# Two transformer blocks: the first projections start from columns loaded as such, and the long convolution's tiles are split five and three

## The chip, the cores and the metric

The kernel runs on one core of one Trainium2 chip. The metric is the device time of one execution in microseconds (us). TensorE is PE in the profile (PEld its weight loads), VectorE is DVE, ScalarE is ACT, GpSimd is POOL, and SP issues most DMAs.

## The reference

Two blocks of 256 tokens and width 1024, in fp32. Cut to what the change touches:

```python
# block one
xn = rms_norm(x, norm1_g)                       # x * rsqrt(mean(x^2) + eps) * g
proj = xn @ w_in                                # q, keys and values, g_nsa, conv_b, conv_c, conv_x, gate_a, gate_b
u = conv_c * conv_x
y = causal_conv(u, conv_w)                      # 3 taps, each channel by itself
z = conv_b * y
mixed = sigmoid(gate_a) * (o_nsa @ w_branch_a) + sigmoid(gate_b) * (z @ w_branch_b)
# block two, the branch with the long convolution
u = a * sigmoid(gate)
u = causal_conv(u, conv_w_2) + conv_b_2         # 31 taps, each channel by itself
u = silu(layer_norm(u)); y_conv = u @ w_conv_out
```

## The kernel before

**Products in parts.** Every fp32 product is made of three fp32r ones. ScalarE rounds an operand to fp32r (the hi part, by `copy`, L916), VectorE subtracts it from the original (the lo part, L1435 for weights, L1494 for tokens), and TensorE sums hi x hi, hi x lo and lo x hi (`mm`, L400).

**Units.** All weights come in 302 units of mostly two k-tiles x 512 columns (512 KB), in the fixed order of `units`. SP loads a unit into one of five `raw` buffers as soon as the lo part of the unit five before it is made, ScalarE makes `whi`, VectorE `wlo`, each in rings of five, and TensorE uses them. `rows` puts tokens on the output's partitions (12 matmuls of 512 columns for a unit), `cols` channels (24 of 256 columns). Two to four PSUM banks take a group's tiles; a bank is used again when its tile has been copied out (`bank_free`), by ScalarE for the groups in `by_act` and by VectorE for the others.

**Order.** Each engine runs a program written out by hand. `run(name, ...)` on ScalarE and VectorE makes the hi or lo parts up to four units ahead, and the generators given to it (attention, conv taps, norms) do one step per unit. Engines work in program order, so whatever stands ahead of a hi or lo part delays it.

**The start.** The tokens `X` are loaded first, then unit 0, and TensorE transposes the raw tokens (L404, 16 transposes, zero matmuls before, between and after them). ScalarE and VectorE make the hi and lo parts of these columns times the gain in `OT`. The groups `b1_q`, `b1_kv` (four units of 512 columns each) and `b1_w` (four of 280) run on these unscaled columns, and `copy_out` puts the norm's factor in afterwards, row by row. The factor comes from ScalarE's four squares (L961), VectorE's mean (L1465, L1467) and a power on GpSimd (L2105). VectorE scales the rows into `XS`, and TensorE transposes them too, four transposes after each unit of `b1_kv` (`turn_first`). All later groups of block one (`b1_c0`, `b1_x0`, `b1_c1`, `b1_x1`, `b1_b0`, `b1_b1`, the gates) run on these scaled columns in `XT`.

**Convolution of block one.** ScalarE copies the tiles of `b1_c0` and `b1_c1` out (`copy_col`) into `CC`, and VectorE multiplies the tiles of `b1_x0` and `b1_x1` by them (`col_product`, L1712).

**The long convolution.** Of its eight tiles of 128 channels VectorE makes four (`PE_CONV`), 31 taps each (`taps2`, L1838 and L1842), spread over the units: two taps a unit for 24 units, then three. TensorE makes the other four (`conv_taps`) as 32 matmuls of 32 x 32 tiles each, from a shifted copy `U4` that comes by 16 DMAs, and blocks `WQ` that VectorE makes. One tile is done after every second unit. When all eight are in `YC`, VectorE sums them (L1858), and TensorE needs that sum for the layer norm's mean.

```python
if q == 0: wait_bank(name, f)                             # cols, TensorE, before a tile's first matmul
e.wait_ge(factor, t + 1)                                  # ScalarE, ahead of each copy_out of the first groups
```

## Time and profile before

| what | us |
|---|---|
| runs before: median (lowest to highest of 3) | 943.23 (942.1 to 943.39) |
| the profiled execution, its own time | 942.65 |
| its span, first to last instruction | 940.8 |
| PE busy | 932.1 |
| DVE busy | 671.5 |
| ACT busy | 523.3 |
| POOL busy | 15.2 |

The profiled execution's time is 1.85 us above its span. Busy time is a share of the whole span: PE is busy for 99% of it, DVE for 71%, ACT for 56%, and the mean hides stages in which DVE is busy nearly throughout. The mean DMA rate is 178 GB/s over the span.

### The profile page before, as it was taken

Reading aid. Unit: us, or ns where it says so; the run is one execution under the profiler, and the core shown is the slowest. Engines: PE = TensorE matmul, PEld = TensorE weight load, DVE = VectorE, ACT = ScalarE, POOL = GpSimd, SP = SyncE. Lnnn points to the kernel's source line nnn. Section 1 sums busy time; section 2 is a strip of 40 time slices with the busy share of each in tenths; the row PEclk is TensorE's granted clock in tenths of the full one; section 3 lists DMA queues with packets and bytes.
Section 4 is the critical chain, followed back from the end, with each engine's and each line's share of the span. In section 5 each row is a group of like instructions: output and inputs, shape, how many; then the busy total and the mean of one; then the engine's idle time right before and its main releaser. Section 6 shows DMA issues by size and latency. Waiting matters only on the chain.

```text
span 940.8 us, 14580 instructions
## 1 busy us (share of the span) xinstructions
PE 932.1 (99%) x5619; PEld 802.7 (85%) x5619; DVE 671.5 (71%) x1142; ACT 523.3 (56%) x897; POOL 15.2 (2%) x20
## 2 busy tenths in 40 slices
PE   9999999999999999999999999999999999999997
PEld 7999987788888888889999988888788888888886
DVE  5669976477776666667568876999786676666665
ACT  6655677745654544555444435664855664555453
...
PEclk9999999999999999999999999999999999999999
...
DMA packets 89540, 167.06 MB, mean 178 GB/s; under 512 B 7616, under 2 KB 12416, under 8 KB 89344
## 3 DMA queue, kind: packets, MB, share of 16 engines
...
q14 instruction: 23, 0.19, 0.1%
...
HBM read 162.68 MB, written 1.05 MB: 174 GB/s over the span
## 4 chain that ended last, share of the span: by engine, by line
PE 95%; ACT 2%; DVE 1%; issue 1%; POOLq 0%; POOL 0%; DVEq 0%; ACTq 0%
PE pb L400 92%; PE pb L404 3%; ACT whi L916 1%; ACT YC L1233 0%; DVE LNS L1858 0%; ACT ZO L916 0%; ACT GA L1056 0%; ACT L1233 0%; ACT L1056 0%; DVE GA L1725 0%; DVE XS L2069 0%; ACT S L1372 0%; DVE wlo L1435 0%; ACT GC L1056 0%; DVE ZO L1494 0%
## 5 line engine op out<-in xcount | busy, mean ns | idle before, releaser
L1435 DVE TENSOR_TENSOR wlo<-raw,whi 128x1024 fp32r<-128x1024 f32 (+2 forms) x300 | 357.5, 1213 | 157.3 <-ACT whi L916 156.4
L916 ACT ACTIVATE whi<-raw 128x1024 fp32r<-128x1024 f32 (+2 forms) x302 | 310.2, 1047 | 162.4 <-PE pb L400 147.2
L400 PE MATMUL pb<-XT,whi 128*128 128x256 f32 (+1 forms) x1552 | 372.8, 323 | 0.0
L400 PE MATMUL pb<-XT,wlo 128*128 128x256 f32 (+1 forms) x1032 | 290.6, 282 | 0.0
L400 PEld LDWEIGHTS pb<-XT,whi 128*128 128x128 f32 x1552 | 257.6, 190 | 28.6 <-issue 3.8
L400 PE MATMUL pb<-whi,ZO 128*128 128x512 f32 (+2 forms) x904 | 280.3, 387 | 0.9 <-DVE wlo L1905 0.6
L400 PEld LDWEIGHTS pb<-whi,ZO 128*128 128x128 f32 x904 | 168.4, 188 | 36.4 <-DVE wlo L1435 1.6
L400 PEld LDWEIGHTS pb<-XT,wlo 128*128 128x128 f32 (+1 forms) x1032 | 195.8, 190 | 0.5
L400 PE MATMUL pb<-wlo,ZO 128*128 128x512 f32 (+2 forms) x452 | 173.7, 384 | 0.0
L400 PE MATMUL pb<-whi,XT 128*128 128x512 f32 x448 | 150.8, 401 | 0.0
L400 PEld LDWEIGHTS pb<-whi,XT 128*128 128x128 f32 x448 | 84.2, 188 | 18.3 <-issue 1.3
L400 PEld LDWEIGHTS pb<-wlo,ZO 128*128 128x128 f32 x452 | 85.0, 188 | 16.0
L400 PE MATMUL pb<-wlo,XT 128*128 128x512 f32 x224 | 87.5, 391 | 0.0
L1842 DVE SCALAR_TENSOR_TENSOR YC<-U,PR,YC 128x256 f32<-128x256 f32 x120 | 51.4, 478 | 0.0
L400 PEld LDWEIGHTS pb<-wlo,XT 128*128 128x128 f32 x224 | 42.2, 189 | 7.6
L916 ACT ACTIVATE RT<-pb 128x256 f32<-128x256 f32 x64 | 24.0, 375 | 40.5 <-PE pb L400 40.5
L1762 DVE TENSOR_TENSOR HF<-pb,RT 128x256 f32<-128x256 f32 x64 | 26.9, 420 | 24.8 <-ACT RT L916 24.8
L916 ACT ACTIVATE ZO<-HF 128x256 fp32r<-128x256 f32 x64 | 26.8, 419 | 25.0 <-DVE HF L1765 23.3
L1765 DVE SCALAR_TENSOR_TENSOR HF<-HF 128x256 f32<-128x256 f32 x64 | 27.2, 426 | 2.2
L1754 DVE TENSOR_TENSOR ZO<-HF,ZO 128x256 fp32r<-128x256 f32 x64 | 26.9, 420 | 2.4 <-ACT ZO L916 1.1
L2105 POOL TENSOR_TENSOR ST<-ST,CST 128x1 f32<-128x1 f32 (+3 forms) x14 | 13.7, 986 | 916.5 <-DVE ST L1467 682.5
L1122 ACT ACTIVATE SM<-SM,ST 128x128 f32<-128x128 f32 (+1 forms) x48 | 21.4, 447 | 11.9 <-DVE ST L1581 11.8
...
## 6 DMA issues: line engine op xcount, KB each, us to landing
raw<-in_w_in SPq DMA_DIRECT2D x107, 512.0 KB, 4.2
raw<-in_w_ff SPq DMA_DIRECT2D x64, 512.0 KB, 4.5
raw<-in_w_up SPq DMA_DIRECT2D x32, 512.0 KB, 4.3
raw<-in_w_down SPq DMA_DIRECT2D x32, 512.0 KB, 4.6
raw<-in_w_branch_b SPq DMA_DIRECT2D x8, 512.0 KB, 4.5
raw<-in_w_out SPq DMA_DIRECT2D x8, 512.0 KB, 5.1
raw<-in_wx_kv SPq DMA_DIRECT2D x8, 512.0 KB, 5.0
raw<-in_w_attn_out SPq DMA_DIRECT2D x8, 512.0 KB, 3.5
```

The lines of the kernel that those rows point to most:

```text
L400: return e.matmul(o, l, r, start=start, stop=stop, skip_group_check=True)
L404: return e.transpose(o, s, ident[0:n, 0:n])
L916: return e.activation(o, i, ACT.Copy, scale=scale)
L1122: i = e.activation(SM[j % 4][:, c0:c1], SM[j % 4][:, c0:c1], ACT.Exp, bias=INM[j % 4][:, t:t + 1], scale=post, accum_out=ISM[j % 4][:, t:t ...
L1435: e.tensor_tensor(wlo[u % NW][:, 0:c], raw[u % NRAW][:, 0:c], whi[u % NW][:, 0:c].bitcast(F32), ALU.subtract).then_inc(lo, 1)
L1754: e.tensor_tensor(ZT[:, a + 256:a + 512], HF[:, f, :], ZT[:, a:a + 256].bitcast(F32), ALU.subtract).then_inc(h_lo, 1)
L1762: e.tensor_tensor(HF[:, f, :], PB[bank_of[name, f]][:, 0:256], RT[:, m % 2, :], ALU.add).then_inc(out_d, 1)
L1765: e.scalar_tensor_tensor(out=HF[:, f, :], in0=HF[:, f, :], scalar=0.0, in1=HF[:, f, :], op0=ALU.max, op1=ALU.mult).then_inc(h_sq, 1)
L1842: m = e.scalar_tensor_tensor(out=YC[:, f, :], in0=U2[:, f, k:k + 256], scalar=prm("convw2", 8 * k + f), in1=YC[:, f, :], op0=ALU.mult, op1 ...
L2105: return e.tensor_tensor(dst, src, mhalf(rows, n), ALU.pow)
```

## The change

**The start.** The host also gives the tokens as columns (`xt`). SP loads them in three parts into `XF`, between the first units; `X` itself now comes after unit 4, and the constants come in one piece ahead of unit 4. ScalarE and VectorE make the hi and lo parts in `XT` from `XF`. All 32 transposes of tokens are gone, as are the scaled rows; five zero matmuls are left. For the first three units `first_rows` takes hi and lo parts as they are made. ScalarE squares `X` only after the hi part of unit 6, and then waits for the factor.

**The factor.** Block one runs on unscaled columns throughout. Conv_b and the gates get the factor later (`copy_out` with a scale, `times` with a scalar). Conv_c x conv_x needs it squared, per token, along the columns: VectorE puts 1/mean on diagonals (`DR`), one matmul of 256 columns turns them into rows, and VectorE multiplies the tiles of `b1_c0` and `b1_c1` by them (`RX`) in place of ScalarE's copies. These two groups leave `by_act`, so that their banks now come free by VectorE.

**The long convolution.** VectorE makes five tiles, TensorE three. The taps are spread anew: three a unit for 8 units, two for 15, six for 7, then three; the last step has two in place of one.

```diff
-T_X0, T_X, T_M1, T_MEM, T_2, T_MIX, T_M2, T_XA, T_FFN = range(9)
+T_X, T_M1, T_MEM, T_2, T_MIX, T_M2, T_XA, T_FFN = range(8)
...
-PE_CONV = 4
+SCALED = {n: i for i, n in enumerate((N_MEM, N_MIX))}
+GAIN = {T_X: "norm1", T_MEM: "normmem", T_2: "norm2", T_MIX: "normmix", T_XA: "normx", T_FFN: "normffn"}
+PE_CONV = 5
...
-by_act = {"b1_q", "b1_kv", "b1_w", "b1_c0", "b1_c1", "b1_gb0", "b1_gb1", "b1_ga0", "b1_ga1", "mk", "mv",
+by_act = {"b1_q", "b1_kv", "b1_w", "b1_gb0", "b1_gb1", "b1_ga0", "b1_ga1", "mk", "mv",
...
+    def load_columns(i):
+        a, b = ((0, 512), (512, 1024), (1024, 2048))[i]
+        e.dma_start(XF[:, a:b], A["xt"][:, a:b]).then_inc(xt_in[i], 16)
+
+    load_columns(0)
+    for k in range(2):
+        e.dma_start(raw[0][:, 512 * k:512 * k + 512], units[0][0][0][0][:, k, :]).then_inc(raw_in[0] if k else first_in, 16)
+    load_columns(1)
+    load(1)
+    load_columns(2)
+    load(2)
+    load(3)
+    e.dma_start(CST[:, :], A["consts"]).then_inc(cst_in, 16)
+    load(4)
     for t in range(2):
         e.dma_start(X[:, t * D:t * D + D], xv[:, t, :]).then_inc(x_in[t], 16)
-    for k in range(2):
-        e.dma_start(raw[0][:, 512 * k:512 * k + 512], units[0][0][0][0][:, k, :]).then_inc(raw_in[0] if k else first_in, 16)
-    load(1)
-    e.dma_start(CST[:, 128:CS["end"]], A["consts"][:, 128:CS["end"]]).then_inc(cst_in, 16)
-    for u in range(2, NRAW):
-        load(u)
     e.dma_start(PR[:, 8:NPRM], A["params"][:, 8:NPRM]).then_inc(prm_in, 16)
...
                 e.dma_start(U4[32 * j:32 * j + 32, :, g, a:284],
-                            U2[32 * g:32 * g + 32, 4:8, j + a - 1:j + 283]).then_inc(u4_in, 16)
+                            U2[32 * g:32 * g + 32, PE_CONV:8, j + a - 1:j + 283]).then_inc(u4_in, 16)
...
+    def first_rows(name, T):
+
+        for u in range(count[name] - 1):
+            h, l = weight_tiles(u)
+            for k in range(2):
+                kt = 2 * u + k
+                e.wait_ge(*((first_k, 1) if kt == 0 else (hi, u + 1)))
+                for part in range(2):
+                    e.wait_ge((t_hi, t_lo)[part], kt + 1)
+                    for t in range(2):
+                        a = kt * 512 + part * 256 + t * P
+                        mm(PB[bank_of[name, t]][:, :], T[:, a:a + P], h[:, k, :], kt == 0 and part == 0, False)
+            for k in range(2):
+                kt = 2 * u + k
+                e.wait_ge(*((first_k, 2) if kt == 0 else (lo, u + 1)))
+                for t in range(2):
+                    a = kt * 512 + t * P
+                    i = mm(PB[bank_of[name, t]][:, :], T[:, a:a + P], l[:, k, :], False, False)
+            i.then_inc(unit_done, 1)
...
-    def turn_first():
-        for j in range(4):
-            rows_scaled(N_X, j)
-            turn_tiles(T_X, j, XS, (t_lo, t_at[T_X0, j]))
-            yield
+    def factor_rows():
+        yield
+        yield
+        e.wait_ge(cst_in, 16)
+        e.wait_ge(dr_made, 2)
+        mm(PB[4][:, 0:256], ones, DR[:, :], True, True).then_inc(rx_done, 1)
+        yield
 
...
-        for n in range(4):
+        for n in range(8 - PE_CONV):
...
-    def busy(n):
-        for _ in range(n):
-            mm(PB[3][:, 0:256], DG[:, 0:128], DG[:, 0:256], True, True)
-
     e.wait_ge(zeros, 1)
-    busy(6)
-    e.wait_ge(id_in, 16)
-    for t in range(2):
-        e.wait_ge(x_in[t], 16)
-        for j in range(4):
-            for k in range(2):
-                c = t * D + (2 * j + k) * P
-                i = turn(PB[4 + j][:, k * 256 + t * P:k * 256 + t * P + P], X[:, c:c + P])
-            if t:
-                i.then_inc(turned, 1)
-        busy(1 if t == 0 else 3)
-    side = turn_first()
-    rows("b1_q", OT, t_ready(T_X0))
-    rows("b1_kv", OT, t_ready(T_X0), side)
-    rows("b1_w", OT, t_ready(T_X0))
+    for _ in range(5):
+        mm(PB[3][:, 0:256], DG[:, 0:128], DG[:, 0:256], True, True)
+    first_rows("b1_q", XT)
+    rows("b1_q", XT, t_ready(T_X), begin=3)
+    rows("b1_kv", XT, t_ready(T_X), factor_rows())
+    rows("b1_w", XT, t_ready(T_X))
...
-    make_t_hi(T_X0, 0, OT)
-    for k in range(2):
-        e.wait_ge(raw_in[0] if k else first_in, 16)
-        copy(whi[0][:, 512 * k:512 * k + 512], raw[0][:, 512 * k:512 * k + 512]).then_inc(
-            *((hi, 1) if k else (first_k, 1)))
-    made[0] = 1
-    for j in range(1, 4):
-        make_t_hi(T_X0, j, OT)
-        make_hi()
-    for t in range(2):
-        e.wait_ge(x_in[t], 16)
-        for i in range(2):
-            norm_square(N_X, X, i, t)
+    for j in range(4):
+        e.wait_ge(xt_in[min(j, 2)], 16)
+        for kt in (2 * j, 2 * j + 1):
+            copy(XT[:, kt * 512:kt * 512 + 256], XF[:, kt * 256:kt * 256 + 256], prm(GAIN[T_X], kt)).then_inc(t_hi, 1)
+        for k in range(2) if j == 0 else ():
+            e.wait_ge(raw_in[0] if k else first_in, 16)
+            copy(whi[0][:, 512 * k:512 * k + 512], raw[0][:, 512 * k:512 * k + 512]).then_inc(
+                *((hi, 1) if k else (first_k, 1)))
+        if j == 0:
+            made[0] = 1
+        else:
+            make_hi()
     for n, (name, c0, w) in enumerate((("b1_q", 0, 512), ("b1_kv", 512, 512), ("b1_w", 1024, 280))):
-        run(name, *([turn_first()] if n == 2 else []))
+        run(name)
+        for t in range(2) if n == 0 else ():
+            e.wait_ge(x_in[t], 16)
+            for i in range(2):
+                norm_square(N_X, X, i, t)
         for t in range(2):
             e.wait_ge(factor, t + 1)
             copy_out(name, t, QKV[:, t, c0:c0 + w], NR[N_X][t])
...
     side = attention1()
     for i in range(2):
         run(f"b1_c{i}", side)
-        for f in range(4):
-            if i == 1:
-                e.wait_ge(qk_t, 6)
-            copy_col(f"b1_c{i}", f, CC[i][:, f, :])
         run(f"b1_x{i}", side)
...
-                    copy_out(f"b1_{nm}{i}", t, g)
+                    copy_out(f"b1_{nm}{i}", t, g, NR[N_X][t])
...
+            if n is None:
+                e.tensor_tensor(g, PB[bank_of[name, t]][:, :], g, ALU.mult).then_inc(out_d, 1)
+            else:
+                e.scalar_tensor_tensor(out=g, in0=PB[bank_of[name, t]][:, :], scalar=NR[n][t], in1=g,
+                                       op0=ALU.mult, op1=ALU.mult).then_inc(out_d, 1)
...
     def conv_blocks():
-        for n in range(4):
+        for n in range(8 - PE_CONV):
...
     def taps2():
-        n, made = 0, {}
-        for f0 in range(0, PE_CONV, 2):
+
+        places = itertools.chain(*([q] * n for q, n in enumerate((3,) * 8 + (2,) * 15 + (6,) * 7 + (3,) * 20)))
+        made, at = {}, 0
+        for fs in ((0, 1), (2, 3, 4)):
             for k in range(31):
-                for f in (f0, f0 + 1):
+                for f in fs:
+                    q = next(places)
+                    while at < q:
+                        at += 1
+                        yield
                     if k == 0:
...
-                    n += 1
-                    if n % (2 if n < 48 else 3) == 0:
-                        yield
...
-    make_t_lo(T_X0, 0, OT)
+    def make_x_lo(j):
+        for kt in (2 * j, 2 * j + 1):
+            a = kt * 512
+            e.wait_ge(t_hi, kt + 1)
+            e.scalar_tensor_tensor(out=XT[:, a + 256:a + 512], in0=XF[:, kt * 256:kt * 256 + 256],
+                                   scalar=prm(GAIN[T_X], kt), in1=XT[:, a:a + 256].bitcast(F32), op0=ALU.mult,
+                                   op1=ALU.subtract).then_inc(t_lo, 1)
+
+    make_x_lo(0)
...
-    norm_rows(N_X, X, XS)
     run("b1_q")
+    e.wait_ge(cst_in, 16)
+    for t in range(2):
+        mean(N_X, t, 2 + 2 * t)
+        e.wait_ge(summed, t + 1)
+        step(e.reciprocal(NSUM[N_X][t], NMEAN[N_X][t]))
+        after_step()
+        e.tensor_scalar(DR[:, t * P:t * P + P], ident, NSUM[N_X][t], None, ALU.mult).then_inc(dr_made, 1)
     head_mean(0)
     run("b1_kv")
+    e.wait_ge(rx_done, 1)
+    e.tensor_copy(RX[:, :], PB[4][:, 0:256]).then_inc(rx_out, 1)
     head_mean(1)
     head_scale(0)
-    run("b1_w", turn_first())
+    run("b1_w")
     head_mean(2)
     head_scale(1)
     side = attention1()
     taps = []
     for i in range(2):
         run(f"b1_c{i}", side, *taps)
+        e.wait_ge(*((qk_t, 6) if i else (rx_out, 1)))
+        for f in range(4):
+            col_product(f"b1_c{i}", f, CC[i][:, f, :], RX[:, :])
         run(f"b1_x{i}", side, *taps)
         now(*taps)
...
-    times("b1_wb0", GB, 0, gate_made(2))
+    times("b1_wb0", GB, 0, gate_made(2), N_X)
...
+    xt = I["x"].reshape(256, 8, P).transpose(2, 1, 0).reshape(P, 2048)
+    arrays = {"xt": xt, "params": params, "consts": c, "consts2": c2, "wcmp": wcmp, "x": I["x"], "mem_2": I["mem_2"],
```

ScalarE from the last columns' hi parts on. Before:

```order
L916 ACTIVATE ZO<-pb,PR 128x256 x2
L916 ACTIVATE whi<-raw 128x1024
L961 ACTIVATE XS,ST<-X 128x512 x4
L916 ACTIVATE whi<-raw 128x1024 x3
L916 ACTIVATE QKV<-pb,ST 128x512 x2
L1073 ACTIVATE SQ<-QKV 128x1024
L916 ACTIVATE whi<-raw 128x1024
```

Now (lines are those of the changed kernel):

```order
L940 ACTIVATE XT<-XF,PR 128x256 x2
L940 ACTIVATE whi<-raw 128x1024 x4
L985 ACTIVATE XS,ST<-X 128x512 x4
L940 ACTIVATE QKV<-pb,ST 128x512 x2
L1092 ACTIVATE SQ<-QKV 128x1024
```

The four squares of `X` (output `XS`) moved behind the hi parts of units 4, 5 and 6, to just ahead of the first copies out, which need the factor. The next hi part, that of unit 7, stands behind them as before.

VectorE at the end of `b1_c1` (SM are attention's scores, CC the tiles of conv_c). Before:

```order
L1573 SCALAR_TENSOR_TENSOR SM<-pb,CST 128x384
L1578 TENSOR_REDUCE ST<-SM 128x1 x2
L1581 TENSOR_SCALAR ST<-ST 128x2
L1435 TENSOR_TENSOR wlo<-raw,whi 128x1024
L1698 TENSOR_SCALAR CC<-UU,PR 128x256
```

Now:

```order
L1585 SCALAR_TENSOR_TENSOR SM<-pb,CST 128x384
L1590 TENSOR_REDUCE ST<-SM 128x1 x2
L1593 TENSOR_SCALAR ST<-ST 128x2
L1724 TENSOR_TENSOR CC<-pb,RX 128x256 x4
L1452 TENSOR_TENSOR wlo<-raw,whi 128x1024
```

The four products that release the banks of `b1_c1` stand behind the scores of two heads, and ahead of the next unit's lo part.

VectorE in the units before attention's second part (YC are the taps). Before:

```order
L1842 SCALAR_TENSOR_TENSOR YC<-U,PR,YC 128x256 x2
L1435 TENSOR_TENSOR wlo<-raw,whi 128x1024
L1842 SCALAR_TENSOR_TENSOR YC<-U,PR,YC 128x256 x3
L1435 TENSOR_TENSOR wlo<-raw,whi 128x1024
L1842 SCALAR_TENSOR_TENSOR YC<-U,PR,YC 128x256 x3
```

Now:

```order
L1865 SCALAR_TENSOR_TENSOR YC<-U,PR,YC 128x256 x6
L1452 TENSOR_TENSOR wlo<-raw,whi 128x1024
L1865 SCALAR_TENSOR_TENSOR YC<-U,PR,YC 128x256 x2
L1861 TENSOR_SCALAR YC<-U,PR 128x256 x3
L1865 SCALAR_TENSOR_TENSOR YC<-U,PR,YC 128x256
```

Seven units in a row have six taps each where one had two and six had three.

## Rows read from the trace of the kernel before

**Rows 1.** The page: PE's busy time, and the clock granted in 40 slices.

```profile
PE 932.1 (99%) x5619; PEld 802.7 (85%) x5619; DVE 671.5 (71%) x1142; ACT 523.3 (56%) x897; POOL 15.2 (2%) x20
...
PEclk9999999999999999999999999999999999999999
```

**Rows 2.** Waits of PE: engine line <- releaser: us in total, times, longest.

```profile
PE pb L400 <- DVE wlo L1435: 0.4, 1, 0.4
...
PE pb L400 <- DVE LNS L1858: 0.3, 1, 0.3
```

**Rows 3.** Timeline of PE, first 11 us: start us, us, engine, line, instruction [idle before].

```profile
1.19 5.12 PE L400 MATMUL pb<-DG 128*128 128x256 f32 x12 [1.19 <-DVE DG L1899]
...
8.33 1.46 PE L400 MATMUL pb<-DG 128*128 128x256 f32 x6
10.34 0.50 PE L400 MATMUL pb<-whi,ZO 128*128 128x512 f32 x1 [0.55 <-DVE wlo L1905]
```

**Rows 4.** Chain that ended last, 31 to 34 us: start us, us, what.

```profile
31.05 2.75 PE pb L400 x12
33.80 0.44 PE pb L404 x4
```

**Rows 5.** DMA in 0:8, 8:20, and what 12:13.5 issued (KB, us to landing).

```profile
DMA packets 1155, 2.26 MB, mean 282 GB/s; under 512 B 238, under 2 KB 366, under 8 KB 1155
...
DMA packets 2010, 4.68 MB, mean 390 GB/s; under 512 B 130, under 2 KB 258, under 8 KB 1901
...
raw<-in_w_in SPq DMA_DIRECT2D x1, 512.0 KB, 4.6
```

**Rows 6.** Timeline of ACT, 8 to 23 us.

```profile
8.67 1.15 ACT L916 ACTIVATE whi<-raw 128x512 fp32r<-128x512 f32 x2
...
14.69 0.67 ACT L961 ACTIVATE XS<-X 128x512 f32<-128x512 f32 x1
...
17.14 2.98 ACT L916 ACTIVATE whi<-raw 128x1024 fp32r<-128x1024 f32 x3
20.25 0.69 ACT L916 ACTIVATE QKV<-pb,ST 128x512 f32<-128x512 f32 x1
...
22.33 1.06 ACT L1073 ACTIVATE SQ<-QKV 128x1024 f32<-128x1024 f32 x1
```

**Rows 7.** Timeline of DVE, 18 to 25 us.

```profile
18.58 1.29 DVE L1477 TENSOR_SCALAR XS<-X,ST 128x512 f32<-128x512 f32 x3 [0.45 <-POOL ST L2105]
...
23.43 1.22 DVE L1602 TENSOR_REDUCE ST<-SQ 128x16 f32<-128x1024 f32 x1 [0.16 <-ACT SQ L1073]
```

**Rows 8.** Timeline of ACT, last tile of b1_c1.

```profile
83.48 0.38 ACT L916 ACTIVATE CC<-pb 128x256 f32<-128x256 f32 x1 [0.34 <-PE pb L400]
```

**Rows 9.** Timeline of DVE, 84 to 86 us.

```profile
84.12 0.17 DVE L1581 TENSOR_SCALAR ST<-ST 128x2 f32<-128x2 f32 x1
84.84 1.22 DVE L1435 TENSOR_TENSOR wlo<-raw,whi 128x1024 fp32r<-128x1024 f32 x1 [0.56 <-ACT whi L916]
```

**Rows 10.** Groups of PE, 486 to 700 us: xcount | busy us, mean ns | idle.

```profile
L400 PE MATMUL pb<-ZO,WQ 128*32 128x256 f32 x256 | 14.6, 380 | 0.0
```

**Rows 11.** Timeline of DVE, 549 to 575 us.

```profile
549.77 1.27 DVE L1842 SCALAR_TENSOR_TENSOR YC<-U,PR,YC 128x256 f32<-128x256 f32 x3
554.45 1.22 DVE L1435 TENSOR_TENSOR wlo<-raw,whi 128x1024 fp32r<-128x1024 f32 x1 [3.41 <-ACT whi L916]
...
567.70 1.23 DVE L1435 TENSOR_TENSOR wlo<-raw,whi 128x1024 fp32r<-128x1024 f32 x1 [4.38 <-ACT whi L916]
...
573.54 1.23 DVE L1435 TENSOR_TENSOR wlo<-raw,whi 128x1024 fp32r<-128x1024 f32 x1 [3.49 <-ACT whi L916]
```

**Rows 12.** Busy us of PE, PEld, DVE, ACT in 600 to 620 us.

```profile
600.00:620.00 20.00, 20.00 (x101) 16.79 (x100) 19.26 (x43) 13.05 (x32) 0.00 (x0) 1.00 0.53 150
```

**Rows 13.** Timeline of DVE, the norm's first sum.

```profile
642.15 3.82 DVE L1858 TENSOR_REDUCE LNS<-YC 128x256 f32<-128x2048 f32 x1
```

**Rows 14.** Timeline of PE, the matmul on it.

```profile
646.03 0.70 PE L400 MATMUL pb<-LNS,CST 128*128 128x256 f32 x2 [0.26 <-DVE LNS L1858]
```

60 lines of the change are left out of this document (26 added, 34 removed).

## The prediction

> **What bounds the kernel now.** I read the page first, then PE's waits, the chain of waits, and the timelines of the places that the change touches. The page shows TensorE busy for 932.1 of 940.8 us at the full clock [rows 1]; its waits inside the program are tenths of a microsecond [rows 2]. So the kernel is bound by TensorE. Work taken off it, or an earlier first matmul, shortens the time, but only as far as the engines that feed it keep up. A wait shorter than half a microsecond is a near tie: there the other engine is the next bound. Matmuls on data begin at 10.34 us [rows 3].
>
> **The start.** Three costs go from TensorE.
>
> (a) The first matmul no longer waits for transposes. It needs the first columns and gains, two hi parts of columns (0.7 us together) and half a unit's hi part (0.6 us, from two in 1.15 us [rows 6]). Ten passes of zero matmuls end at 1.19 + 4.27 = 5.5 us [rows 3]; by then the first quarter of the columns, now first in the queue, should have landed. I put the first matmul at about 5.8 us, 4.6 us sooner, as an estimate.
>
> (b) The 16 transposes of scaled rows, four times 0.44 us [rows 4], are gone: 1.7 us.
>
> (c) The matmul that turns the factor adds 0.4 us, by the two passes of 256 columns of [rows 14].
>
> If nothing else waited, the start would give 4.6 + 1.7 - 0.4 = 5.9 us. I don't forecast that, for ScalarE and the DMA can't follow. The tokens travel twice, and `X` is now ahead of units 5 and 6. Up to unit 6 the queue holds columns 1.05, seven units 3.67, constants 0.54, `X` 1.05 and parameters 0.26 MB, 6.57 MB in all. By 8 us 2.26 MB had moved, afterwards 390 GB/s [rows 5], so the last byte moves at 8 + 4.31 / 0.390 = 19.0 us. Before, unit 6 stood behind 5.52 MB, which by the same count were moved at 16.4 us; it was issued at about 12.8 and landed 4.6 us later [rows 5], 1.0 us behind its bytes. So unit 6 lands at 20.1 us.
>
> From there ScalarE works in order: hi part 1.0 us (three in 2.98), the four squares 2.45 (14.69 to 17.14), the factor 1.45 (17.14 to the scaling at 18.58), the second copy out 0.7, head squares 1.06 [rows 6, 7]. Then VectorE sums them (1.3 us [rows 7]) and makes unit 7's lo part (1.2 us [rows 9]). That is 20.1 + 1.0 + 2.45 + 1.45 + 0.7 + 1.06 + 1.3 + 1.2 = 29.3 us. TensorE wants unit 7 at about 27 us and waits two microseconds. Before, unit 7 began at 31.05 and had 0.44 us of transposes behind it [rows 4]. The gain at the end of `b1_kv` is 31.05 - 29.3 + 0.44 = **2.2 us**. Unit 5 (landed at 19) also comes late, by a good microsecond; that wait is taken up in the same sum, as is the factor's matmul. A slower first matmul changes nothing up to some 3 us. Ends of this term: 0 (each step a little later, as where the DMA gives 350 GB/s) and 5.9 us.
>
> What is removed here from VectorE (eight lo parts, four scalings) and ScalarE (eight hi parts) was covered by TensorE and counts for nothing; from `b1_w` on it gives both engines slack.
>
> **The tiles of conv_c.** Eight copies of 0.38 us leave ScalarE and eight products reach VectorE. The four of `b1_c0` find VectorE with the time it saved on lo parts; I take them at nothing. If that cover were gone they would cost up to 0.8 us. The four of `b1_c1` stand behind two heads' scores. Before, the last tile was complete at 83.44, just ahead of its copy, and ScalarE had freed the first one's bank two microseconds sooner [rows 8]; VectorE left the scores at 84.29 [rows 9]. In these times, leaving the start's shift aside, the first bank now comes free one product (0.42 us) later, at 84.7, and the first matmul of `b1_x1` on that bank wants it at 83.44. Behind it is queued all of TensorE's program. Cost: **+1.3 us**, between 0 and 1.8. The other products follow every 0.36 us and TensorE needs a bank only every 0.72 us. VectorE is nearly full for 25 us after this place, but TensorE is then later by more than VectorE, so I add nothing. The other factors ride on copies and products that exist already: nothing.
>
> **The long convolution.** TensorE loses one tile of four, 14.6 / 4 = 3.65 us [rows 10], on the path. VectorE gets 31 taps and loses one block of weights (1.2 us). Three taps take 1.27 us with the tail of the last, some 0.39 each [rows 11]: 12.2 us more. Eight taps fall on the first eight units, where VectorE waited for ScalarE for more than that. Twenty-two fall on seven units between 547 and 575 us: 8.7 us. There VectorE waited too; the three longest waits alone are 3.41 + 4.38 + 3.49 = 11.3 us [rows 11]. But these waits end when TensorE frees a buffer or ends a tile, and TensorE is 3.65 us earlier there, so about 9.5 of 13 us are usable. The taps just fit. This is the closest cover of the change: afterwards VectorE is busy for 19.26 of 20 us [rows 12], so what does not fit would be handed to TensorE at the layer norm. One tap more stands directly ahead of the sum over the tiles (3.82 us [rows 13]), on which TensorE waited 0.26 us already [rows 14]: 0.4 us are given back. Net **3.65 - 0.4 = 3.25 us**. Ends: 3.65, and below nothing if the taps don't fit. The copies of `U4` shrink by a quarter; TensorE did not wait for them, so nothing.
>
> **Sum.** -2.2 + 1.3 - 3.25 = -4.15 us against the profiled execution's 942.65 us: 938.5 us. That execution is 0.6 us below the median of the runs shown, 943.23; from the median it would be 939.1. I say 938.7. What a measurement of this kernel can tell from no change is 0.2%, 1.9 us.
>
> **A rule that speaks against it.** TensorE's clock: the 12 passes of zero matmuls took 5.12 us, 0.43 us each, the 1.2 GHz level, although the page's slices show full clock; the six at 8.33 took 0.22 us each but for the last one's tail, the 2.4 GHz level [rows 3]. No wait in this trace is as long as the two that I expect before units 5 and 7. The Trainium skill, "TensorE: Matmul & The Clock Gate" (What's actually happening), says that the throttled state is the default and activity releases it. By that rule TensorE could fall back in these waits; the trace can't show it, and it makes the first rival below.
>
> **Rivals.**
>
> *The clock falls in the waits at the start.* Then some 5.1 us after unit 7's wait run at half speed, as the first 5.12 us did, and cost 2.6 us. For it: the new idle stretches of one and two microseconds, and zero matmuls that were placed between the transposes are gone. Against it: a wait of 0.55 us changed nothing [rows 3], and the matmuls between the waits are dense. A fall at the first wait would be hidden in unit 7's. 941.2 us, chance 0.10.
>
> *The feeding keeps up.* If the DMA moves faster in the new order, or the squares and the factor hide, unit 7 is ready when wanted, and the start gives 5.9 us: 942.65 - 5.9 + 1.3 - 3.25 = 934.8 us. Against it: every term of the chain has its row. 0.09.
>
> *VectorE becomes the bound of block two.* If the 8.7 us of taps before 575 us are not hidden, the sum over the tiles is 8.7 + 0.4 us later, less some 2.8 us in which VectorE still waits up to there: TensorE reaches the layer norm 6.3 us later than before in place of 3.25 us earlier. -2.2 + 1.3 + 6.3 = +5.4: 948 us, **slower**. It decides from 4.2 us of taps on that are not hidden. For it: VectorE's share in [rows 12], and that in its program a lo part stands behind every six taps. Against it: the waits in [rows 11]. 0.09. If 2 to 4 us are not hidden, the gain of the tile is lost and the time is about 941.5: 0.12.
>
> *The change doesn't do what it says*: the slice of gains lands as late as before, behind more data, and the first matmul stays late. The start is then unchanged in its effect, since unit 7 decides: inside the forecast.
>
> **How the numbers follow.** The forecast's mechanism with its sizes off by a microsecond either way (936.5 to 940.7) has 0.60. The likeliest time is 938.7. The range 936.0 to 942.0 holds this case, the clock's and the half-hidden taps; most of the other 0.18 lies outside. Faster by over 0.2% are the forecast (0.60), the better feeding (0.09) and a few hundredths of the middle cases: 0.72. Within 0.2%: the rest of those, 0.19. Slower: 0.09.
>
> **What would show it.** Right: the first matmul on data near 6 us; ScalarE's squares after 21 us; PE waiting about 2 us on a lo part at 27 to 29 us, and 1.3 us on VectorE's CC product near 82 us; the matmuls on WQ at 11 us; PE's wait on the sum over the tiles 0.3 to 0.8 us. Wrong: no wait before unit 7 (the start is better), passes of 0.43 us after it (the clock), or waits of several microseconds on VectorE between 570 and 650 us.

## The result and the profile after

| | before | changed |
|---|---|---|
| median of 7 runs each | 942.97 us (942.04 to 943.57) | 939.44 us (939.12 to 940.98) |
| the profiled execution, its own time | 942.65 | 939.12 |
| its span | 940.8 | 937.3 |

The ratio is 0.9966, 95% interval 0.9954 to 0.9977: 3.5 us faster, where 4.3 were forecast (938.7 us). A second measurement, among the experiments, gave 938.98 against 942.50, 3.5 us again.

The page and the waits of TensorE in the changed kernel (engine, line, releaser: us in total, times, longest):

```profile
PE 923.2 (98%) x5515; PEld 795.0 (85%) x5515; DVE 681.2 (73%) x1173; ACT 520.1 (55%) x880; POOL 14.9 (2%) x20
```

```profile
PE pb L414 <- DVE wlo L1452: 3.2, 3, 1.8
PE pb L414 <- issue: 1.3, 1, 1.3
PE pb L414 <- ACT whi L940: 1.3, 1, 1.3
...
PE pb L414 <- DVE LNS L1878: 0.6, 1, 0.6
```

TensorE's busy time fell by 8.9 us, the span by 3.5: the waits took most of the difference. Against [rows 2] three waits are new: on lo parts, on a hi part, and one that the profile calls "issue". The timeline of PE in the changed kernel tells their places:

```profile
1.19 3.88 PE L414 MATMUL pb<-DG 128*128 128x256 f32 x10 [1.19 <-DVE DG L1919]
6.33 2.11 PE L414 MATMUL pb<-whi,XT 128*128 128x512 f32 x8 [1.26 <-ACT whi L940]
...
21.78 0.50 PE L414 MATMUL pb<-whi,XT 128*128 128x512 f32 x1 [0.98 <-DVE wlo L1452]
...
29.75 0.50 PE L414 MATMUL pb<-whi,XT 128*128 128x512 f32 x1 [1.78 <-DVE wlo L1452]
...
81.42 0.28 PE L414 MATMUL pb<-XT,wlo 128*128 128x256 f32 x1
83.04 0.48 PE L414 MATMUL pb<-XT,whi 128*128 128x256 f32 x2 [1.34 <-issue]
...
642.33 0.70 PE L414 MATMUL pb<-LNS,CST 128*128 128x256 f32 x2 [0.64 <-DVE LNS L1878]
```

Matmuls on data begin at 6.33 us, 4.0 us sooner than in [rows 3]. Unit 7 begins at 29.75. In the timeline of PE in the kernel before it began at 30.80:

```profile
30.80 0.47 PE L400 MATMUL pb<-whi,ZO 128*128 128x512 f32 x1
```

The chain of [rows 4] puts this at 31.05, because a piece of the chain starts where the piece before it ends. With the 0.44 us of transposes that stood behind the unit, 30.80 + 0.44 - 29.75 = 1.5 us of the start's gain are left at the end of `b1_kv`. The rest went into the two waits at 21.78 and 29.75.

The same instructions of TensorE, by their starts in the two timelines, give a balance by place:

| place | before | changed | shift |
|---|---|---|---|
| first matmul of `b1_w` on a lo part | 34.20 | 32.72 | -1.5 |
| first transposes of attention one | 46.20 | 44.52 | -1.7 |
| transposes behind the first unit of `b1_x1` | 86.10 | 85.98 | -0.1 |
| the 16 transposes ahead of block two's columns | 433.18 | 432.89 | -0.3 |
| transposes behind the long convolution | 587.61 | 583.54 | -4.1 |
| the matmul on the norm's sum | 646.03 | 642.33 | -3.7 |
| span | 940.8 | 937.3 | -3.5 |

By attention one the start has won 1.7 us, the tiles of conv_c lose 1.6, the long convolution wins 3.8 and loses 0.4 at the norm. Another 0.2 us are won between 86 and 433 us, and 0.2 lost behind 692 us. The wait for the bank costs more than its 1.34 us of idle time: a matmul in the flow starts some 0.16 us before the one ahead of it has ended, and from 81.42 to 83.04 there are 1.62 us where these matmuls follow each other every 0.12.

What makes unit 7 late stands in the timeline of ACT, and in that of DVE (two last lines):

```profile
4.85 0.91 ACT L940 ACTIVATE XT<-XF,PR 128x256 fp32r<-128x256 f32 x2 [2.16 <-DMA PR<-in_params]
...
19.40 1.06 ACT L940 ACTIVATE whi<-raw 128x1024 fp32r<-128x1024 f32 x1 [3.54 <-DMA raw<-in_w_in]
20.76 1.06 ACT L940 ACTIVATE whi<-raw 128x1024 fp32r<-128x1024 f32 x1 [0.29 <-DMA raw<-in_w_in]
21.72 0.61 ACT L985 ACTIVATE XS<-X 128x512 f32<-128x512 f32 x1
...
26.04 1.06 ACT L1092 ACTIVATE SQ<-QKV 128x1024 f32<-128x1024 f32 x1
```

```profile
27.14 1.22 DVE L1614 TENSOR_REDUCE ST<-SQ 128x16 f32<-128x1024 f32 x1 [1.96 <-ACT SQ L1092]
...
28.47 3.19 DVE L1452 TENSOR_TENSOR wlo<-raw,whi 128x1024 fp32r<-128x1024 f32 x4
```

Units 5 and 6 come out of the DMA at 19.40 and 20.7 us. ScalarE then squares the tokens, copies out twice and squares the heads; VectorE sums those and only then makes unit 7's lo part, which was 1.8 us overdue. Ahead of the first data stands the slice of gains: ScalarE waited for it until 4.85. The DMA itself was behind by then; the views of DMA in the changed kernel, 0 to 8 and 8 to 20 us:

```profile
DMA packets 1078, 1.93 MB, mean 241 GB/s; under 512 B 224, under 2 KB 224, under 8 KB 1078
...
DMA packets 2051, 4.76 MB, mean 397 GB/s; under 512 B 158, under 2 KB 286, under 8 KB 2051
```

In the first 8 us it moved 0.33 MB less than in [rows 5], and afterwards slightly more per microsecond.

The place of conv_c and block two's taps, in the timeline of DVE, with the groups of PE between 480 and 700 us (busy us, mean ns) and a window of 600 to 620 us (busy us of PE, PEld, DVE, ACT, POOL, then PEclk, DMA share, GB/s):

```profile
82.51 1.41 DVE L1724 TENSOR_TENSOR CC<-pb,RX 128x256 f32<-128x256 f32 x4
...
554.15 1.23 DVE L1452 TENSOR_TENSOR wlo<-raw,whi 128x1024 fp32r<-128x1024 f32 x1 [2.44 <-ACT whi L940]
...
569.46 1.23 DVE L1452 TENSOR_TENSOR wlo<-raw,whi 128x1024 fp32r<-128x1024 f32 x1 [0.97 <-ACT whi L940]
...
638.48 3.80 DVE L1878 TENSOR_REDUCE LNS<-YC 128x256 f32<-128x2048 f32 x1
```

```profile
L414 PE MATMUL pb<-ZO,WQ 128*32 128x256 f32 x192 | 11.0, 380 | 0.0
```

```profile
600.00:620.00 20.00, 20.00 (x100) 16.78 (x100) 19.79 (x45) 11.72 (x29) 0.00 (x0) 1.00 0.53 157
```

VectorE reaches the four products of `b1_c1` at 82.51, when the softmax of two heads is through; its first product, a quarter of these 1.41 us, ends just before TensorE goes on at 83.04. The matmuls on WQ fell from 14.6 [rows 10] to 11.0 us. The three longest waits of VectorE between 549 and 575 us were 11.3 us in all [rows 11]; now two are left, 3.4 us. The taps fit.

### The profile page after: what moved, and what is told of

Its sections match the earlier page's. It is cut to its first block, busy times and chain, and to the rows that moved or that the text cites. A ratio compares the mean times of both kernels' runs of the same rounds, so it can differ in the third digit from the quotient of the medians.

```text
span 937.3 us, 14384 instructions
## 1 busy us (share of the span) xinstructions
PE 923.2 (98%) x5515; PEld 795.0 (85%) x5515; DVE 681.2 (73%) x1173; ACT 520.1 (55%) x880; POOL 14.9 (2%) x20
## 4 chain that ended last, share of the span: by engine, by line
PE 92%; ACT 3%; DVE 2%; DMA 2%; issue 1%; SPq 0%; POOL 0%; POOLq 0%; DVEq 0%
PE pb L414 89%; PE pb L418 3%; DMA raw<-in_w_in 2%; ACT whi L940 1%; DVE wlo L1452 1%; ACT YC L1252 0%; DVE LNS L1878 0%; ACT XS L985 0%; ACT ZO L940 0%; ACT GA L1075 0%; ACT L1252 0%; ACT L1075 0%; DVE GA L1739 0%; DVE ST L1614 0%; ACT S L1389 0%
## 5 line engine op out<-in xcount | busy, mean ns | idle before, releaser
L414 PE MATMUL pb<-whi,ZO 128*128 128x512 f32 (+1 forms) x808 | 253.1, 390 | 0.4 <-DVE wlo L1452 0.4
L414 PE MATMUL pb<-whi,XT 128*128 128x512 f32 (+1 forms) x544 | 176.4, 394 | 4.1 <-DVE wlo L1452 2.8
L414 PEld LDWEIGHTS pb<-whi,ZO 128*128 128x128 f32 x808 | 151.2, 188 | 33.1 <-DVE wlo L1452 1.6
L414 PE MATMUL pb<-wlo,ZO 128*128 128x512 f32 (+1 forms) x404 | 156.5, 387 | 0.0
L414 PEld LDWEIGHTS pb<-whi,XT 128*128 128x128 f32 x544 | 101.2, 188 | 26.7 <-DVE wlo L1452 4.3
L414 PE MATMUL pb<-wlo,XT 128*128 128x512 f32 (+1 forms) x272 | 103.2, 385 | 0.0
L414 PEld LDWEIGHTS pb<-wlo,ZO 128*128 128x128 f32 x404 | 75.9, 188 | 14.8
L1865 DVE SCALAR_TENSOR_TENSOR YC<-U,PR,YC 128x256 f32<-128x256 f32 x150 | 63.4, 477 | 0.0
L414 PEld LDWEIGHTS pb<-wlo,XT 128*128 128x128 f32 x272 | 51.3, 188 | 8.8
L2144 POOL TENSOR_TENSOR ST<-ST,CST 128x1 f32<-128x1 f32 (+3 forms) x14 | 13.5, 971 | 917.9 <-DVE ST L1484 687.5
```

What stands on the lines that cost most here:

```text
L414: return e.matmul(o, l, r, start=start, stop=stop, skip_group_check=True)
L1865: m = e.scalar_tensor_tensor(out=YC[:, f, :], in0=U2[:, f, k:k + 256], scalar=prm("convw2", 8 * k + f), in1=YC[:, f, :], op0=ALU.mult, op1 ...
L2144: return e.tensor_tensor(dst, src, mhalf(rows, n), ALU.pow)
```

## The experiments

All times are medians, each against runs of the kernel before on the same chip in the same sequence. That kernel's median was 942.37 us for the first four experiments; 942.57 for the one without zero matmuls, the even taps and the two further edits of the start; 942.66 for the fill by six and the split six and two; and 942.50 for the fill by three and the changed kernel again. Beside the changed kernel's first runs it was 942.97. So times of different sequences compare to some 0.6 us at best, and the difference to the kernel before is the better measure: 3.5 us for the changed kernel, both times.

### The changed kernel with four and four tiles

```diff
-PE_CONV = 5
+PE_CONV = 4
...
-    (3,) * 8 + (2,) * 15 + (6,) * 7 + (3,) * 20
+    (2,) * 24 + (3,) * 26
-    for fs in ((0, 1), (2, 3, 4)):
+    for fs in ((0, 1), (2, 3)):
```

> The changed kernel with the long convolution split four and four and its taps spread as before. Theory: the start's gain (1.7 us at the end of b1_kv) and the wait at b1_c1 (1.6 us) cancel, and the fifth tile carries the whole result; so this run is within 0.5 us of the kernel before (about 942.6 in the profile, span 940.7), unit 7 still begins near 29.7 us and b1_x1 waits 1.3 us. Rival: the start carries its share, and the run stays at 940 to 941.

Measured: 943.2 us, ratio 1.0008 (0.9999 to 1.0017), 0.8 us above the kernel before, where at most 0.5 either way was expected. The start and the factor together gain nothing. 1.7 us won and 1.6 lost would leave nothing either; the next experiment shows where some of the 0.8 may come from. The profiled execution took 944.16 us, one of the two longest of eleven, and shows something that the changed kernel's profile doesn't: behind unit 7's wait the matmuls run at half speed. The timeline of PE here (the changed kernel ran the same pair, with two and one pass, in 0.61 and 0.39 us):

```profile
29.46 0.50 PE L414 MATMUL pb<-whi,XT 128*128 128x512 f32 x1 [1.79 <-DVE wlo L1452]
...
31.07 1.05 PE L414 MATMUL pb<-whi,XT 128*128 128x512 f32 x2
31.92 0.63 PE L414 MATMUL pb<-wlo,XT 128*128 128x512 f32 x1
```

and the window of 30 to 33.6 us, of this kernel and then of the changed one (the last three numbers are PEclk, DMA share and GB/s):

```profile
30.00:33.60 3.60, 3.60 (x10) 2.76 (x9) 1.72 (x4) 0.69 (x1) 2.79 (x2) 0.55 0.88 279
```

```profile
30.00:33.60 3.60, 3.60 (x20) 3.11 (x20) 2.00 (x4) 1.40 (x3) 3.02 (x2) 1.00 0.78 246
```

Ten passes in place of twenty in the same 3.6 us, at a granted clock of 0.55: the 1.2 GHz level. It cost 1.6 us (16.56 us against 14.94 for the same 108 matmuls). So the rival of the clock is real, in some executions.

### The kernel before with five and three tiles alone

```diff
-PE_CONV = 4
+PE_CONV = 5
+    (3,) * 8 + (2,) * 15 + (6,) * 7 + (3,) * 20
...
-    for n in range(4):
+    for n in range(8 - PE_CONV):
```

> The kernel before with only the five and three split and the new spread of taps. Theory: 3.65 us less TensorE work, 0.4 us given back at the sum over the tiles: 939.3, span 937.4, as fast as the whole change. Rival: the taps fit only because the start gave slack; then 941 or more, with a longer wait of TensorE on the sum.

Measured: 938.85 us, ratio 0.9964 (0.9951 to 0.9976), where the whole change has 0.9966. The long convolution carries all of the result. The wait on the norm's sum is 0.6 us here as well.

This kernel starts as the kernel before does, and its timeline of PE shows how uneven that start is:

```profile
1.19 4.51 PE L401 MATMUL pb<-DG 128*128 128x256 f32 x12 [1.19 <-DVE DG L1903]
...
9.73 0.50 PE L401 MATMUL pb<-whi,ZO 128*128 128x512 f32 x1 [0.55 <-DVE wlo L1909]
```

The same twelve passes took 5.12 us in [rows 3], and data followed at 10.34 us. The first transposes of attention one stand at 45.60 here and at 46.20 in the trace of the kernel before, with nothing changed in between. Against this execution the changed start wins 1.1 us and not 1.7, and with the 1.6 lost at conv_c the start and the factor are a loss of 0.5 us. How often the start is early or late over all executions was not measured. The parts alone, +0.8 and -3.5, add up to -2.7 us and not to -3.5; what remains of this is within the intervals and stays open.

### Unit 7's parts ahead of the squares

```diff
+    if n == 0:
+        owed[0] = 0
+        make_hi()
...
     run("b1_q")
+    owed[0] = 0
+    make_lo()
```

> The changed kernel; ScalarE makes unit 7's hi part ahead of the four squares, VectorE its lo part ahead of the means. Theory: the wait of 1.8 us before unit 7 came from this order; it goes or shrinks below 0.3 us, unit 7 begins near 27.9, and the time falls by 1.5 to 1.8 us to about 937.7. Rival: the DMA sets the pace, unit 7's data come too late or the wait moves to unit 8 or to the first copies out, and the time moves by less than 0.5 us.

Measured: 938.3 us, ratio 0.9953 (0.9941 to 0.9966). The wait at unit 7 is gone, and part of it comes back in `b1_w`, on a lo part that now stands behind VectorE's scaling of the heads:

```profile
36.16 0.40 PE L414 MATMUL pb<-whi,XT 128*128 128x280 f32 x1 [0.64 <-DVE wlo L1455]
```

1.78 us less 0.64 is 1.1 us. In the profiles the first transposes of attention one stand 1.0 us sooner than in the changed kernel (43.55 and 44.52), the matmul on the norm's sum 0.8 sooner (641.57 and 642.33). The median is 1.1 us under the changed kernel's, but the gain over the kernel before is larger by 0.5 us only (4.1 and 3.5), or by 1.2 if taken from the ratios. The 1.5 to 1.8 us that I expected did not come.

### `b1_c1` copied out by ScalarE, multiplied later

```diff
-by_act = {"b1_q", "b1_kv", "b1_w", "b1_gb0", ...
+by_act = {"b1_q", "b1_kv", "b1_w", "b1_c1", "b1_gb0", ...
...
+    e.wait_ge(*out_at["b1_c1", 3])
+    step(e.tensor_tensor(CC[1], CC[1], RX[:, :].unsqueeze(1).broadcast_to([P, 4, 256]), ALU.mult))
```

> The changed kernel; ScalarE copies the tiles of b1_c1 out again, and VectorE multiplies the copies by the factor in one product behind the scores. Theory: the bank was what b1_x1 waited for; the 1.3 us gap at 81.7 us and the slow first unit of b1_x1 (0.2 us) go, time 937.9. Rival: TensorE waits for VectorE there in any case (for the next lo part or for attention's scores), as VectorE has no less to do: the gap only moves, less than 0.5 us gained.

Measured: 938.23 us, ratio 0.9952 (0.9939 to 0.9966). The "issue" wait is gone; the chain of waits runs through the place as it did before the change (start us, us, what):

```profile
63.84 20.60 PE pb L414 x184
```

The transposes behind the first unit of `b1_x1` stand at 84.28 in place of 85.98, those of attention one at 44.38 in place of 44.52: 1.6 us are won between the two, all that conv_c had cost. So that wait was for a bank that VectorE's product frees, although the profile names no releaser.

### No zero matmuls

```diff
-for _ in range(5):
+for _ in range(0):
     mm(PB[3][:, 0:256], DG[:, 0:128], DG[:, 0:256], True, True)
```

> The changed kernel without any zero matmuls ahead of the first matmul on data. In the changed kernel they took 3.88 us (10 passes from 1.19 us on) and the first matmul on data stood at 6.33 us, set by its hi part. Theory (the start is bounded by ScalarE's chain, not by TensorE): the first matmuls begin at about 6.3 us as before, but at 0.43 us a pass for some 4 to 5 us, which makes TensorE about 2 us later at unit 5; the waits before units 5 and 7 (0.98 and 1.78 us in the changed kernel) shrink by as much, and the matmuls after unit 7's wait begin at 29.7 us as in the changed kernel. Time 939.4 us, within 0.5. Rival (the clock falls in the waits and the zero matmuls protect it): a lower granted clock at some place between 20 and 36 us, passes of 0.43 us there, and 941 to 942 us in most executions. A lower clock there in the profile of the kernel with four and four tiles (passes of 0.43 us for 3.6 us behind unit 7's wait, in one of its slower executions) is why this is asked.

Measured: 939.39 us (939.00 to 940.79), ratio 0.997 (0.9959 to 0.9981): no difference in the median. The first eight passes take 3.75 us (0.43 us each) where they took 2.11, the wait at unit 5 is gone, and unit 7 begins where it did:

```profile
6.06 3.75 PE L414 MATMUL pb<-whi,XT 128*128 128x512 f32 x8 [6.06 <-ACT whi L940]
...
29.61 0.50 PE L414 MATMUL pb<-whi,XT 128*128 128x512 f32 x1 [1.80 <-DVE wlo L1452]
```

TensorE lost 1.6 us in these passes and unit 7 did not move: the start is bounded by what feeds unit 7. The rival was half right. In the profiled execution (940.63 us) the clock fell behind unit 7's wait again (0.58 between 30 and 33.6 us); of the seven executions this one and one more (940.79) lie over a microsecond above the median.

### The taps spread evenly

```diff
-(3,) * 8 + (2,) * 15 + (6,) * 7 + (3,) * 20
+(3,) * 45 + (4,) * 5
```

> The changed kernel with its 155 taps spread evenly: three behind each of 45 units and four behind the last five, in place of 3, 2, 6 and 3. Fifteen more taps (5.9 us of VectorE at 0.39 us each) fall between 494 and 545 us, where VectorE is busy for 14.19 of 15, 13.56 of 15 and 9.79 of 10 us in the changed kernel; 21 fewer (8.2 us) between 547 and 575 us, where it waited 2.4 and 1.0 us. Theory (where the taps stand decides, VectorE has room behind 547 us and not ahead of it): 2 to 4 us of the taps don't fit and TensorE waits for lo parts between 515 and 547 us by 1 to 3 us; the sum over the tiles ahead of the layer norm comes later by 0 to 1 us because of the two more taps near the end: 941 to 943 us. Rival (VectorE has room all over, since its buffers are ahead): no wait of TensorE above 0.3 us before the layer norm, 939.4 us within 0.5.

Measured: 942.02 us (940.27 to 943.59), ratio 0.9992 (0.9984 to 1.0001). Of the 3.5 us 0.6 are left (942.57 to 942.02). But not for the reason that I expected: there is no wait of TensorE between 515 and 547 us, although VectorE is busy for 15.00 of 15 us from 500 to 515 us. So the fifteen taps more in the middle cost nothing, as the rival had it. The price is paid at the norm, on the sum over the tiles (timeline of PE), and behind it (window):

```profile
643.77 0.70 PE L414 MATMUL pb<-LNS,CST 128*128 128x256 f32 x2 [1.96 <-DVE LNS L1878]
```

```profile
646.00:649.00 3.00, 3.00 (x10) 2.38 (x9) 3.00 (x2) 0.78 (x1) 0.00 (x0) 0.62 0.80 273
```

1.96 us in place of 0.64, and then the lower clock level once more. What makes the sum late stands in the timeline of DVE, with the same scores of attention two in the changed kernel (first line) and here:

```profile
620.32 0.55 DVE L1585 SCALAR_TENSOR_TENSOR SM<-pb,SC 128x384 f32<-128x384 f32 x1
```

```profile
569.57 1.23 DVE L1452 TENSOR_TENSOR wlo<-raw,whi 128x1024 fp32r<-128x1024 f32 x1 [3.56 <-ACT whi L940]
...
620.44 0.55 DVE L1585 SCALAR_TENSOR_TENSOR SM<-pb,SC 128x384 f32<-128x384 f32 x1
...
634.21 1.67 DVE L1865 SCALAR_TENSOR_TENSOR YC<-U,PR,YC 128x256 f32<-128x256 f32 x4
...
640.05 3.67 DVE L1878 TENSOR_REDUCE LNS<-YC 128x256 f32<-128x2048 f32 x1
```

VectorE had caught up long before the norm: it waited 3.56 us for ScalarE at 569 us, and at 620 us it is 0.1 us behind the changed kernel, as TensorE is from the start on. Between 620 us and the sum it then makes 23 taps where the changed kernel has 17: four behind each of the last five units in place of three, and of two behind the last. Six taps are 2.3 us; 0.7 of them fall into a wait for TensorE (that of `GA` at 635 us), and the sum starts 1.57 us later (638.48 there). The expectation had counted two more taps near the end and put 0 to 1 us on them. So this run shows what six taps directly ahead of the sum cost, and nothing about a lack of room ahead of 547 us.

### The wait at the norm filled

The fills go ahead of the matmul on the sum, into a bank that this matmul overwrites; nothing else is changed from the even taps.

```diff
+    for _ in range(6):
+        mm(PB[7][:, 0:256], DG[:, 0:128], DG[:, 0:256], True, True)
     e.wait_ge(ln_tiles, 1)
```

> The kernel with the taps spread evenly, and six zero matmuls (12 passes of 256 columns, some 0.11 us each at full clock, 1.3 us in all) ahead of the matmul on the sum over the tiles, inside the 1.96 us that TensorE waits there. In the profile of the even taps the 3.6 us behind that wait ran at the 1.2 GHz level and took 1.7 us more than the same matmuls in the changed kernel. Theory (the idle time lets the clock fall): the wait shrinks to some 0.7 us, the clock stays at its upper level behind it, the matmul on the sum stays where it is (643.8 us), and the time goes from 942.0 to 940.4 us. Rival (the fall has nothing to do with the wait, or the fill is not enough): 942.0 us within 0.4, passes of 0.43 us behind 644 us.

Measured: 941.28 us, ratio 0.9986 (0.9977 to 0.9995). The fill was twice as long as I had put it:

```profile
641.82 2.76 PE L414 MATMUL pb<-DG 128*128 128x256 f32 x12
644.41 0.60 PE L414 MATMUL pb<-LNS,CST 128*128 128x256 f32 x2
```

The matmul on the sum is 0.64 us later than without a fill, and yet the kernel is faster, since the clock stayed up behind it. With three zero matmuls in place of six:

> As the filled kernel, with three zero matmuls in place of six. The 12 passes took 2.61 us (641.82 to 644.41, 0.22 us each) and not 1.3, so that the matmul on the sum came 0.64 us late; six passes take 1.3 us and leave some 0.7 us of the wait. Theory (idle time of about 2 us in one piece lets the clock fall, a shorter piece does not): the matmul on the sum back at 643.8 us, a wait of 0.6 to 0.7 us ahead of it, the upper clock level behind it, and 940.6 us; that is 0.6 under the filled kernel (941.28) and 1.4 under the unfilled one (942.02). Rival (only a full fill holds the clock): 942.0 us, passes of 0.43 us behind 644 us.

Measured: 940.54 us, ratio 0.9984 (0.9975 to 0.9993).

```profile
641.73 1.46 PE L414 MATMUL pb<-DG 128*128 128x256 f32 x6
643.88 0.70 PE L414 MATMUL pb<-LNS,CST 128*128 128x256 f32 x2 [0.69 <-DVE LNS L1880]
```

As the theory of the clock had it: the matmul on the sum starts within 0.1 us of where it did, behind 0.69 us of idle time in place of 1.96, and the median is 1.5 us lower. The median alone is weak evidence. The two kernels ran on different chips, their ratios to the kernel before differ by 0.0008 only, 0.8 us, and the intervals overlap. The single executions say more, since the mean granted clock goes with the time:

| kernel | single executions, us (mean granted clock) |
|---|---|
| even taps | 940.27, 940.41, 941.00 (0.999); seven from 941.87 to 942.43 (0.997); 943.59 (0.995) |
| filled by six | eight from 940.95 to 941.47 (0.998 to 1.0); 942.59, 942.72, 943.17 (0.997) |
| filled by three | eight from 940.31 to 940.81 (0.999 or 1.0); 941.84, 942.04, 942.31 (0.997) |

The steps between the groups are about 1.6 us, what one fall of the clock cost where a profile has it. By that reading, unfilled, eight of eleven executions had at least one; filled, three of eleven each, where unit 7's wait of 1.8 us is left. One execution of the unfilled kernel has the clock and the time of two falls. The three unfilled executions at the upper level are as fast as those filled by three: the fill gains nothing but the fall that it prevents. Where the clock fell in an execution without a profile is inferred from its time and mean clock, not seen.

### The changed kernel again

> The changed kernel once more, beside the former on the same chip. Either theory: 939.4 us, within 0.4. Its wait of 1.8 us ahead of unit 7 stands, so the theory of the clock expects a few executions about 1.5 us above the rest; without a link between the wait and the clock none would be above the rest by more than before's are above theirs.

Measured: 938.98 us (938.77, 938.80, 938.98, 939.48, 940.44), ratio 0.9967 (0.9954 to 0.9979). One of five lies 1.5 us above the median, as one of seven did in the first measurement (940.98). That fits the clock, but the mean clock of 0.998 doesn't set this one apart, so it is not shown for it. Nor does a late execution need a fall: one of the kernel before, which has no such wait, took 944.64 us at a mean clock of 1.0, 2.0 us above its median.

### Loads and unit 7 first, then both edits

```diff
     load(4)
+    for u in (5, 6):
+        e.wait_ge(lo, u - NRAW + 1)
+        load(u)
     for t in range(2):
         e.dma_start(X[:, t * D:t * D + D], xv[:, t, :]).then_inc(x_in[t], 16)
```

> The changed kernel with unit 7's hi and lo parts ahead of the squares and means, and with the loads of units 5 and 6 issued ahead of the row copy of the tokens. Theory (the start is bounded by the order of the loads and of ScalarE's work): the waits before units 5 and 7 (0.98 and 1.78 us) are both gone; of their 2.8 us some comes back as a wait in b1_w on later units' lo parts, as 0.64 us did with unit 7 first alone. The squares move later by the row copy's 1 to 2 us and so does the factor, which the keys and values of block one need, so VectorE's head sums come later. Time 937 to 938 us; against unit 7 first alone (938.3) a gain of 0.5 to 1 us. Rival (the DMA's rate is the bound of the start): the waits come back in full between 30 and 42 us, 938.3 us or more.

Measured: 938.26 us, ratio 0.9955 (0.9942 to 0.9969). Both waits are gone, but this is no better than unit 7 first alone (938.3): waits of 0.39, 0.53 and 0.65 us have come between 26 and 37 us. The time is the rival's, though only 1.6 of the 2.8 us came back. The first of the three waits is on the factor's diagonals (`DR`), which are made 0.3 us later than with unit 7 first alone (26.51 and 26.24), the other two are on lo parts of `b1_w`; whether the order or the DMA's rate bounds the start now was not separated.

With the edit of `b1_c1` on top:

> The former and, with it, b1_c1 copied out by ScalarE and multiplied later in one product. If the two waits are independent, the gain of the c1 edit alone (1.2 us) adds to the former's: 936 to 937 us, and TensorE has no wait above 0.7 us in its program but at most one in b1_w. Rival (taking one wait away uncovers the next): no better than 938.

Measured: **936.71 us** (936.50 to 937.16), ratio 0.9938 (0.9926 to 0.9951). The two edits add: 1.6 us on top of the former's. This is the best version of the study, 5.9 us under the kernel before, where the changed kernel is 3.5 under it. Its waits of PE, the largest:

```profile
PE pb L417 <- DVE wlo L1461: 1.5, 3, 0.6
PE pb L417 <- DVE DG L1928: 1.2, 1, 1.2
PE pb L417 <- ACT whi L943: 0.7, 2, 0.4
```

None inside the program is above 0.64 us, and its five executions lie within 0.7 us.

### Six and two tiles on the best version

```diff
-PE_CONV = 5
+PE_CONV = 6
...
-(3,) * 8 + (2,) * 15 + (6,) * 7 + (3,) * 20
+(6,) * 8 + (2,) * 15 + (7,) * 7 + (3,) * 19 + (2,)
...
-for fs in ((0, 1), (2, 3, 4)):
+for fs in ((0, 1, 2), (3, 4, 5)):
```

> The best version so far (936.7 us) with the long convolution's tiles split six and two: TensorE loses another tile (3.65 us), VectorE gets 31 taps more and one block of weights less (12.2 less 1.2 us): six taps behind each of the first eight units, two behind fifteen, seven behind seven, three behind nineteen and two behind the last. Theory (VectorE is nearly full from 575 us on, 97 of 100, and the changed kernel used up its room): the 24 taps on the first eight units hide (there it waits for ScalarE, 7 us from 470 to 494), the seven at 547 to 575 us take 2.7 of 3.6 us that are left there, but TensorE comes 3.65 us earlier to the layer norm than VectorE can follow: the wait on the sum over the tiles grows from 0.6 to 2 to 4 us, so that 0 to 2 us are gained and up to 1.7 us given back by the clock behind that wait. Time 936.5 us, between 935 and 938. Rival (room up to 640 us is still there): wait below 1 us, 933.2 us. Rival of the other side (the early taps don't hide): waits on lo parts ahead of 547 us, above 938 us.

Measured: 937.3 us, ratio 0.9937 (0.9925 to 0.995): nothing gained by another 3.65 us off TensorE. The time is as expected, its place is not: the wait stands at a softmax ahead of 575 us, and the norm's wait is 0.63 as before. The first row is the timeline of PE, then come windows, and rows of the timeline of DVE:

```profile
573.11 1.42 PE L417 MATMUL pb<-KT,QT 128*128 128x128 f32 x4 [2.17 <-DVE SM L1594]
```

```profile
470.00:494.00 24.00, 24.00 (x203) 23.19 (x201) 24.00 (x50) 10.74 (x20) 0.00 (x0) 1.00 0.53 159
...
573.00:576.00 3.00, 2.89 (x8) 2.38 (x9) 2.97 (x7) 1.93 (x5) 0.00 (x0) 0.56 0.62 175
```

```profile
551.95 1.23 DVE L1461 TENSOR_TENSOR wlo<-raw,whi 128x1024 fp32r<-128x1024 f32 x1 [1.50 <-ACT whi L943]
...
568.49 2.87 DVE L1874 SCALAR_TENSOR_TENSOR YC<-U,PR,YC 128x256 f32<-128x256 f32 x7
...
572.40 0.57 DVE L1594 SCALAR_TENSOR_TENSOR SM<-pb,SC 128x384 f32<-128x384 f32 x1
```

VectorE is busy for 24.00 of 24 us from 470 us on, but that is not what is paid for: at 550 us it waits 1.50 us for ScalarE once more. From 551.95 us on it has no wait, with seven taps and a lo part for each unit (3.9 us), and it reaches the scores at 572.40, while TensorE has nothing else to do from 570.94. The chain that ended last runs through VectorE for these 20 us. The clock falls behind that wait, and wait and fall together (2.2 and 1.6 us) take all that the sixth tile brings. So VectorE is the bound of block two here between 552 and 573 us.

## Why the prediction held, and where it didn't

**The start, -2.2 us: right in mechanism, 0.5 to 0.7 too good.** Measured -1.5 at the end of `b1_kv`, where it was forecast, and -1.7 at attention one. Two terms were off. Unit 7 was put at 29.3 and began at 29.75: unit 6 landed at 20.7 and not at 20.1, ScalarE's and VectorE's links from there took 9.0 us against the 9.2 that I had summed. I had taken the bytes of the first 8 us from the kernel before, 2.26 MB; in the new order they were 1.93, and the missing 0.33 MB are 0.8 us at 397 GB/s. And the 31.05 of [rows 4] that I measured the gain from is the end of the piece before, the unit's own start was 30.80. The 1.7 also owe something to luck: against an execution of the old start that was early itself (9.73 in place of 10.34 us) they would be 1.1. The first matmul on data came at 6.33, not 5.8, since ScalarE waited for the gains until 4.85, and the run without zero matmuls shows that this costs nothing, as "a slower first matmul changes nothing up to some 3 us" had it.

**The tiles of conv_c, +1.3 us: right.** The wait is 1.34 us, at the place and for the reason given. Besides the idle time a wait costs the overlap of two matmuls, some 0.2 us here, which I hadn't counted: +1.6 in all. The products of `b1_c0` cost nothing, as said.

**The long convolution, -3.65 + 0.4 us: right.** Measured -3.8 and +0.4. That the taps fit before 575 us is shown by the profile: VectorE still waits 3.4 us there, and TensorE does not wait. How close the fit is, is shown from one side only. With seven more taps in that stretch and TensorE 3.65 us earlier TensorE waits 2.17 us. The even spread puts fewer taps there and loses its time to six taps ahead of the sum, a cost that the forecast had for one tap (0.4 us).

**The sum.** -1.7 + 1.6 - 3.8 + 0.4 = -3.5 us in the two profiles, -4.15 forecast; the errors are 0.5 at the start and 0.3 at conv_c, both against the forecast, and 0.1 at the convolution for it. What I hadn't seen is how this reads as a whole: two of the three parts cancel, and the long one alone gives the result.

**The rivals.** The clock's, with a chance of 0.10, described one execution rather than the kernel: its price was put at 2.6 us, for 5.1 us at half speed, and is 1.6, for some 3.4; and it is paid in some executions only, so that the median doesn't show it. My argument against it ("the matmuls between the waits are dense") was no protection: they were as dense where the clock fell. The Trainium skill, "TensorE: Matmul & The Clock Gate" (What's actually happening), holds that the throttled state is the default and activity releases it; the falls behind waits of 1.79, 1.80, 1.96 and 2.17 us agree with that, but six of the eight profiles with unit 7's wait show none, and behind waits of 0.6 to 1.34 us no profile does. The better feeding didn't come, since the DMA set unit 6. VectorE as the bound of block two was not reached with five tiles, and was with six. Two prices of that rival don't follow from its own terms: with 8.7 + 0.4 - 2.8 us as the model the sum breaks even at 3.3 us of taps not hidden, not at 4.2, and 2 to 4 us would give 941.4 to 943.4 us, not about 941.5. Neither enters the forecast.
